# First norm and first two projection blocks worked in two token halves

## What is computed

```python
def rms_norm(x, g):
    xf = x.astype(jnp.float32)
    y = xf * lax.rsqrt(jnp.mean(xf * xf, axis=-1, keepdims=True) + EPS)
    return (y * g.astype(jnp.float32)).astype(x.dtype)
...
        h = rms_norm(x, norm1_g[l])
        z = jnp.einsum('bsd,de->bse', h, w_in[l])
        lru_x, lru_gate, sc_b, sc_c, sc_x = jnp.split(z, splits, axis=-1)
        lru_x = causal_dwconv(lru_x, lru_conv_w[l]) + lru_conv_b[l]
```

## Time and profile before

| | |
|---|---|
| median of the runs | 1700.8 us |
| span of the profiled execution | 1699.3 us |
| TensorE busy | 1670.6 us, 98% of the span |
| VectorE, ScalarE, GpSimd busy | 74%, 46%, 27% |
| first matmul of the projections | 26.49 us from the start |
| first matmul of the third block | 50.63 us |

### The profile page before, as it was taken

One profiled execution on the slowest core, in us unless ns is written; L12 is line 12 of the kernel. 1 busy time (PEld: TensorE's weight loads), 2 busy tenths in 40 slices (PEclk: granted clock), 3 DMA queues, 4 the chain that ended last, 5 costly groups with the idle time before them and its releaser, 6 DMA issues.

```text
span 1699.3 us, 20967 instructions
## 1 busy us (share of the span) xinstructions
PE 1670.6 (98%) x7556; PEld 1381.3 (81%) x7556; DVE 1261.6 (74%) x1490; ACT 780.3 (46%) x1048; POOL 451.8 (27%) x270
## 2 busy tenths in 40 slices
PE   6999999999999999999999999999999999999998
PEld 5888878888887888888888888888888888788786
DVE  7577772258999888888888788889827846777654
ACT  5566551225764343434344454555432317566531
POOL 4222222200006455545554000004523342300000
PEclk9999999999999999999999999999999999999999
DMA  8111112143413322222221884852322231020351
GB/s 263 50 37 49 37 50 65 48 166 107 146 69 90 94 74 86 91 82 74 85 83 59 309 306 134 261 189 82 109 87 62 62 111 32 10 78 26 108 224 71
DMA packets 161095, 176.96 MB, mean 104 GB/s; under 512 B 13566, under 2 KB 114692, under 8 KB 161028
## 3 DMA queue, kind: packets, MB, share of 16 engines
q1 hardware_dynamic: 158724, 167.67, 30.6%
q10 hardware_dynamic: 2304, 8.39, 1.3%
HBM read 140.38 MB, written 35.65 MB: 104 GB/s over the span
## 4 chain that ended last, share of the span: by engine, by line
PE 90%; DVE 6%; ACT 2%; issue 1%; DMA 0%; POOL 0%; DVEq 0%
PE ps L950 31%; PE ps L2517 26%; PE ps L2471 19%; PE ps L2763 5%; PE ps L2748 3%; PE ps L2599 1%; PE ps L2802 1%; PE ps L2720 1%; DVE pt_lo L2324 1%; DVE prob L2281 1%; PE ps L2736 1%; DVE square_dve L1707 0%; ACT pt_hi L1606 0%; PE ps L2620 0%; DVE pair_sum L1913 0%
## 5 line engine op out<-in xcount | busy, mean ns | idle before, releaser
L974 POOL TENSOR_TENSOR w_lo<-w_raw,w_hi 128x1024 fp32r<-128x1024 f32 x52 | 134.6, 2591 | 624.9 <-ACT w_hi L1081 624.9
L2517 PE MATMUL ps<-hop_hi_P,wop_hi_P 128*128 128x512 f32 x672 | 263.6, 392 | 3.2 <-DVE u L1924 2.5
L2517 PE MATMUL ps<-hop_lo_P,wop_hi_P 128*128 128x512 f32 x672 | 262.9, 391 | 0.0
L2517 PE MATMUL ps<-hop_hi_P,wop_lo_P 128*128 128x512 f32 x672 | 262.7, 391 | 0.0
L950 PE MATMUL ps<-h_hi,w_hi 128*128 128x512 f32 x720 | 224.1, 392 | 7.5 <-DVE h_lo L1692 6.0
L980 POOL TENSOR_TENSOR wop_lo_P<-pair_sum,wop_hi_P 128x512 fp32r<-128x512 f32 x90 | 136.4, 1516 | 355.4 <-ACT wop_hi_P L1092 355.4
L950 PE MATMUL ps<-h_lo,w_hi 128*128 128x512 f32 x720 | 222.6, 390 | 0.0
L950 PE MATMUL ps<-h_hi,w_lo 128*128 128x512 f32 x720 | 222.2, 390 | 0.0
L950 PEld LDWEIGHTS ps<-h_hi,w_hi 128*128 128x128 f32 x720 | 135.1, 189 | 36.9 <-issue 9.4
L950 PEld LDWEIGHTS ps<-h_lo,w_hi 128*128 128x128 f32 x720 | 135.7, 189 | 28.4
L950 PEld LDWEIGHTS ps<-h_hi,w_lo 128*128 128x128 f32 x720 | 135.7, 188 | 28.3
(11 more groups left out here) (363 smaller groups left out, 3348.9 us busy)
## 6 DMA issues: line engine op xcount, KB each, us to landing
pair_raw<-in_w_up SPq DMA_DIRECT2D x48, 512.0 KB, 4.8
w_raw<-in_w_in SPq DMA_DIRECT2D x46, 512.0 KB, 3.9
dn_raw<-gu_park SPq DMA_DIRECT2D x84, 256.0 KB, 3.9
dn_raw<-in_w_down SPq DMA_DIRECT2D x60, 256.0 KB, 3.1
gu_park<-up_cv SPq DMA_DIRECT2D x24, 512.0 KB, 2.6
out_raw<-in_w_out SPq DMA_DIRECT2D x30, 256.0 KB, 3.1
x_tok<-in_x SPq DMA_DIRECT2D x4, 1024.0 KB, 8.2
x_park<-xs SPq DMA_DIRECT2D x1, 4096.0 KB, 14.3
```

Of the source, the lines that this page charges most:

```text
L974: nc.gpsimd.tensor_tensor(lo[:, :], raw[:, :], hi[:, :].bitcast(f32), ALU.subtract).then_inc(w_lo_done, 1)
L2517: mm = nc.tensor.matmul(dst, w[q][:, k, :], x[q][:, k, :], start=a, stop=b, skip_group_check=True)
```

## The change

The norm and the first two blocks are done for tokens 0 to 511 (`T1`) and then for tokens 512 to 1023 (`T2`).

- SyncE's queue: x parts 0 and 1, the two weight blocks, then x parts 2 and 3. The 16 row transfers go to ScalarE's queue, in front of ScalarE's own work; a square root of a constant stands behind them. The rows now lie in the second half of the `scr` tiles' space, which the `T2` half of the norm uses.
- Factors come in two sets of four token blocks. VectorE squares blocks 0 to 3 first, then 4 and 6 between tiles of `T1`; ScalarE squares 5 and 7.
- Every normed tile, `h_hi` and `h_lo` is made in two halves of 512 tokens.
- TensorE: 32 transposes, the first rows, the first spread, 16 transposes, then block steps of three matmuls for `T1`, with the last 16 transposes, the other rows and the second spread between them, then the steps for `T2`. Block 0 counts as done after its `T2`.
- GpSimd, not ScalarE, rounds the first weight block (`w_hi[0]`).
- The semaphore counts further on (`v_done`, `hi_done`, `rstd_done`, `rb_done`) are shifted to match; the work there is the same.

```diff
+        ROWS_FIRST, ROWS_LATE = 16 * 12, 16 * 4
+        XT_COPIED = (1, 2, 3, 4, 5, 7, 8, 10)
+        FIRST_V, FIRST_LOW = 2 * KT, KT
...
-            for n in range(4):
+            def x_load(n):
                 sp.dma_start(x_tok[:, 2 * n:2 * n + 2, :], x_v[:, 2 * n:2 * n + 2, :]).then_inc(x_in[n], 16)
...
-                sp.dma_start(rows0[row:row + n, 0:P], v).then_inc(rows_in, 16)
...
+            x_load(0)
+            x_load(1)
...
             for b in range(2):
                 load(N_LRU + b, 0, (cols(b, 8, P), w_in_v[:, :, b * D:b * D + P]))
+            x_load(2)
+            x_load(3)
...
-            sp.wait_ge(xt_copied, NT)
+            sp.wait_ge(xt_copied, XT_COPIED[NT - 1])
             sp.dma_start(x_park.rearrange("c p t -> p c t"), xs[:, :, :]).then_inc(x_parked, 16)
...
+            pool.wait_ge(w_in_sem[0], 16)
+            nc.gpsimd.tensor_copy(w_hi[0][:, :], w_raw[0][:, :]).then_inc(w_hi_done, 1)
             low(0)
             low(1)
-            odd_lows(0, lambda c: scr[c % 4][:, :])
+            odd_lows(0, T1)
+            odd_lows(1, T2)
...
+            act.dma_start(rows1[0:72, :], ffn_rows[0:72, :]).then_inc(pos_in, 16)
+            act.dma_start(rows2[0:72, :], ffn_rows[72:144, :]).then_inc(pos_in, 16)
+            act.dma_start(pos_rows_i[0:NT, :], positions_2.rearrange("o (n p) -> (o n) p", p=P)
+                          ).then_inc(pos_in, 16)
+            act.dma_start(freq[:, :], rope_freq).then_inc(pos_in, 16)
+
+            act.wait_ge(const_done, SMALL_CONST)
+            nc.scalar.activation(small[:, 47:48], eps[:, 0:1], ACT.Sqrt).then_inc(sumsq, 1)
 
             def xt_copy(t):
 
                 act.wait_ge(xt_done, t + 1)
-                nc.scalar.copy(xs[:, :, t * P:(t + 1) * P], ps[t % 3][:, :].rearrange("p (c q) -> p c q", c=KT)
-                               ).then_inc(xt_copied, 1)
-
-            for t in range(NT - 2):
...
+            for t in range(3):
                 xt_copy(t)
-
-            act.wait_ge(x_in[3], 16)
-            nc.scalar.activation(scr[4][:, :], x_tok[:, NT - 1, :], ACT.Square,
-                                 accum_out=small[:, NT - 1:NT]).then_inc(sumsq, 1)
-            act.wait_ge(sumsq, 1)
-            act.wait_ge(sumsq_dve, NT - 1)
-            act.wait_ge(const_done, SMALL_CONST)
-            nc.scalar.activation(small[:, 8:16], small[:, 0:8], ACT.Sqrt, bias=eps[:, 0:1],
-                                 scale=1.0 / D).then_inc(root_done, 1)
-            xt_copy(NT - 2)
-            xt_copy(NT - 1)
             act.wait_ge(vec_t, 1)
-            nc.scalar.copy(vec[:, :], ps[3][:, 0:V_COLS]).then_inc(vec_done, 1)
-            high(0)
+            nc.scalar.copy(vec[:, 0:V_ROWS], ps[3][:, 0:V_ROWS]).then_inc(vec_done, 1)
+            token_root(0)
+            xt_copy(3)
+            act.wait_ge(w_hi_done, 1)
             high(1)
-            highs(lambda c: scr[c % 4][:, :], lambda c: (v_done, c + 1))
+            normed_high(0, T1)
+            normed_high(1, T1)
+            xt_copy(4)
+            normed_high(2, T1)
+            normed_high(3, T1)
+            xt_copy(5)
+            normed_high(4, T1)
+            token_square(5, 1)
+            normed_high(5, T1)
+            xt_copy(6)
+            normed_high(6, T1)
+            xt_copy(7)
+            normed_high(7, T1)
+            token_square(7, 2)
+            token_root(1)
+            act.wait_ge(vec_t, 2)
+            nc.scalar.copy(vec[:, V_FFN:V_COLS], ps[3][:, V_FFN:V_COLS]).then_inc(vec_done, 1)
+            for c in range(KT):
+                normed_high(c, T2)
...
+            for t in range(4):
+                token_square(t, t)
+            token_factor(0)
+            dve.wait_ge(pos_in, ROWS_LATE)
             V.tensor_copy(pos_rows[0:NT, :], pos_rows_i[0:NT, :]).then_inc(setup_done, 1)
             dve.wait_ge(vec_done, VEC)
+            dve.wait_ge(xt_copied, XT_COPIED[3])
             dve.wait_ge(rb_done, 1)
-            dve.wait_ge(xt_copied, NT)
-            norm(0, V_NORM1, lambda c: scr[c % 4][:, :], ps[2][:, :], True)
-
+            normed(0, T1)
+            for c in range(KT):
+                if c + 1 < KT:
+                    normed(c + 1, T1)
+                if c % 2 == 0:
+                    even_low(c, T1)
+                if c in (3, 6):
+                    token_square(4 if c == 3 else 6, 4 if c == 3 else 5)
+            token_factor(1)
+            dve.wait_ge(xt_copied, XT_COPIED[NT - 1])
+            dve.wait_ge(rb_done, 2)
+            normed(0, T2)
+            for c in range(KT):
+                if c + 1 < KT:
+                    normed(c + 1, T2)
+                if c % 2 == 0:
+                    even_low(c, T2)
+            dve.wait_ge(vec_done, VEC_ALL)
...
                 if t >= 3:
-                    pe.wait_ge(xt_copied, t - 2)
+                    pe.wait_ge(xt_copied, XT_COPIED[{3: 0, 4: 2, 5: 3, 6: 4, 7: 5}[t]])
...
+            for t in range(4):
+                by_channel(t)
+            pe.wait_ge(rows_in, ROWS_FIRST)
+            by_column(rows0, V_ROWS, 0).then_inc(vec_t, 1)
             pe.wait_ge(rstd_done, 1)
-            spread(ps[2]).then_inc(rb_done, 1)
...
-            first_two(0, (ps[0], ps[1]), 0)
+            spread(ps[3], range(4), HALF).then_inc(rb_done, 1)
+            by_channel(4)
+            by_channel(5)
+
+            def first_step(b, j, t):
+
+                if t is T1 and j == 0:
+                    pe.wait_ge(w_lo_done, b + 1)
+                if b == 0:
+                    pe.wait_ge(lo_dve if j % 2 == 0 else lo_pool, 4 * (t is T2) + j // 2 + 1)
+                wh, wl = blocked(b)
+                for w, x, first, last in ((wh, h_hi, j == 0, False), (wh, h_lo, False, False), (wl, h_hi, False, j == 7)):
+                    mm = nc.tensor.matmul(ps[b][:, t], w[:, j, :], x[:, j, t], start=first, stop=last)
+                if j == 7 and t is T2:
+                    mm.then_inc(block_done, 1)
+
+            def first_blocks(k, t):
+                for b, j in ((0, k), (1, k - 3)):
+                    if 0 <= j < 8:
+                        first_step(b, j, t)
+
+            pe.wait_ge(xt_copied, XT_COPIED[3])
+            for k in range(8 + 3):
+                first_blocks(k, T1)
+                if k == 3:
+                    by_channel(6)
+                elif k == 4:
+                    by_channel(7)
+                elif k == 5:
+                    pe.wait_ge(pos_in, ROWS_LATE)
+                    pe.wait_ge(setup_done, POS_F)
+                    by_column(rows1, 72, V_FFN)
+                    by_column(rows2, 72, V_FFN + 72)
+                    by_column(pos_rows, NT, V_POS).then_inc(vec_t, 1)
+                elif k == 8:
+                    pe.wait_ge(rstd_done, 2)
+                    pe.wait_ge(xt_copied, XT_COPIED[NT - 1])
+                    spread(ps[2], range(4, NT)).then_inc(rb_done, 1)
+            for k in range(8 + 3):
+                first_blocks(k, T2)
```

## The result

The changed kernel takes 1704.9 us (median of 8 runs, 1703.7 to 1706.6) against 1700.8 (8 runs, 1699.7 to 1701.4): a ratio of 1.0026, 95% interval 1.0017 to 1.0035. That is inside the range, but slower by a little more than the 0.2% that I had called no change (the interval reaches down to 0.17%). The mechanism that I forecast took place; 3.3 us came on top of the forecast of 1701.6.

A forecast was written before the change was run, and what follows sets the result against it. TensorE bounds the kernel (90% of 1699.3 us). Third block -0.8 and half clock +1.6 give +0.8, span 1700.1; with the median 1.5 above the span, 1701.6 us, range 1698.3 to 1705.5.

The forecast's parts named there:

- rival B: Slower: TensorE granted half clock through most of T1, about +10 us, 1711; chance 0.12.
- Rival C: Slower: first tile late through GpSimd (+1.9) or rows (+3.6); a 6 us first call would give 1707; chance 0.10.
- half-width operations take 0.68 alone, 0.61 in a row ... 7.4, end at 39.85: VectorE's T2 norm: 8 norm tiles and 4 rests from 32.4 take 7.4 us; parameters then end at 44.6.
- Some 4.4 us early: TensorE at block 1's end is some 4.4 us early, of which 3.6 becomes a new idle stretch.
- 12 tile products ... waits 1.0: 43.5: TensorE's T2: from the first rest at 34.3, products at 0.68 plus waits end block 0 at 43.5.
- +1.6, bounds 0 and 2.7: Half clock on TensorE behind the new idle stretch before the third block costs 1.6 us.
- rival A: Faster: T1 runs without waits, third block at 48.3, clock holds: -2.3, 1698.5; chance beyond 0.2%: 0.10.
- TensorE bridges many short waits at 1.00 between 31.0 and 50.6: Argument for rival A from the trace of before: TensorE's clock holds at 1.00 through short waits.
- No later cover: Behind the third block TensorE is the chain, so the +0.8 there reaches the end: span 1700.1.
- The median's distance from the span: The runs' median lies 1.5 us above the profiled span, turning 1700.1 into 1701.6.
- Rule weighed: VectorE's two squares in T1's waits stand up to 1.2 us each behind GpSimd; otherwise third block 0.4 earlier, 1701.2.
- My 1.3: GpSimd's rounding of w_hi[0] takes 1.3 us, between bounds of 0.95 and 2.34.

The follow-up runs named there:

- both edits: Changed kernel with early parameters, the second half's block 0 ahead of block 1, and the second spread one tile step earlier: 1700.4 us, 0.9999 of the kernel before.
- early parameters: Changed kernel with twelve small parameter operations and the exponential moved ahead of the second half's norm: 1702.7 us, 1.0014 of the kernel before.
- block 0 ahead of block 1: Changed kernel whose second half does all eight tiles of block 0, then all eight of block 1: 1704.5 us, 1.0020 of the kernel before.
- cast late: Changed kernel with VectorE's cast of the positions moved behind the first rest of the first half: 1705.8 us, 1.0031 of the kernel before.
- rows alone: Kernel before with only the 16 row transfers moved from SyncE's to ScalarE's queue, ahead of its copies: 1701.8 us, 1.0008 of the kernel before.
- x first: Changed kernel with all four parts of x asked for ahead of the first weights: 1711.7 us, 1.0069 of the kernel before.
- better version: Both edits, but series steps back behind the second norm, last two squares and second root earlier, second spread at k == 6: 1699.0 us, 0.9992 of the kernel before.
- filled: Changed kernel plus 16 unread matmuls in TensorE's idle stretch before the third block: 1702.3 us, 1.0010 of the kernel before.
- one-tile lag: Kernel before with block 1 following block 0 by one tile instead of three: 1705.5 us, 1.0029 of the kernel before.
- changed again: Changed kernel once more, unchanged, for a second profile: 1704.7 us, 1.0024 of the kernel before.
- better version again: The better version once more, unchanged: 1698.5 us, 0.9988 of the kernel before.

## Why the prediction was right or wrong

**Right: what bounds the start.** First matmul 17.9 (forecast 18.2), second spread ends at 32.3 (32.3), second half's norm at 32.42 (32.4), parameters last, then an idle stretch of 3.68 (3.6) and the clock at 0.50 behind it. The gain in front is given back at the convolution: shown by the version with both edits, which brings 1.8 us at the third block, where early parameters alone bring 0.6 and block 0 ahead of block 1 alone brings nothing that its faster front does not explain. The idle stretch fits because both its ends came 0.9 late: block 1 ended at 47.07 (46.2), the third block began at 50.75 (49.8).

**The time was inside the range by luck.** The range reached up to 1705.5 through a rounding of 2.34 on GpSimd (1.71 measured), the clock at 2.7 (1.6 in the first profile) and a little of rival B, which did not come. What brought the time there were four others, given here for the changed kernel's first profile: 0.9 at the third block, 1.0 around 490 us, 0.8 at 1613 us and 0.5 outside the span. Slower by more than 0.2% had a chance of 0.22, through B and C; neither was the way.

**Wrong by 0.8: "half-width operations take 0.68 alone, 0.61 in a row ... 7.4, end at 39.85".** No row shows the 0.61. Two norm tiles and a rest took 1.40 + 0.69 with small gaps, 2.04 in all or 0.68 each, and four of these 8.2 us until 40.6. In the kernel before, three full-width operations took 3.53 (26.27 to 29.80), 1.18 each: halving the width did not halve the time. The parameters came 0.8 later (45.41). From `half_ba` to `kx` it took 3.4, and `half_ba` ended 1.2 behind its start because of GpSimd, both as forecast.

**A slip in the sum.** Convolution at 44.65 and the same 5.3 behind it give 49.95, not 49.8, and -0.7 instead of -0.8; with the 0.8 above this is the +0.1 that was measured. "Some 4.4 us early" is 4.1 by its own terms.

**Wrong, without effect: "12 tile products ... waits 1.0: 43.5".** Block 0 was ready at about 44.8, as the start of the convolution with early parameters shows, 0.6 ahead of the parameters. **Nor had the sum the cast of the positions**, which stood 2.14 us and moved the first half's norm to 14.90 (forecast 13.6); the run with the cast late shows that this held nothing back but 0.3.

**The clock, "+1.6, bounds 0 and 2.7".** In the first profile exactly 1.6, in others 2.4, 2.6 and 2.7 of the same idle stretch; that the first one hit the number is chance. Filling the stretch takes it away. Of the profiles here, the four with 3.67 or 3.68 us of idle time in front of the third block fell and those with 2.33, 2.70 and 3.04 held, but 1.96 and 2.01 us at 13 to 15 us fell, and 1.78 held. The length of the wait alone does not decide, and I read no threshold from so few executions.

**A row misread in favour of rival A: "TensorE bridges many short waits at 1.00 between 31.0 and 50.6".** That stretch holds no wait; TensorE is busy all through it:

```profile
...
31.00:50.60 19.60, 19.60 (x87) 15.91 (x85) 15.09 (x29) 8.15 (x9) 8.47 (x4) 1.00 0.23 63
...
```

**Missing from the sum: "No later cover".** It holds, but further losses do not follow: +1.0 or +1.5 around 490 us. There TensorE runs at half clock in stretches in every profile of every kernel. They cost as much as in the kernel before in both its profiles and in four others (rows alone, both edits, x first, better version), 1.0 more in four (changed, filled, early parameters, one-tile lag) and 1.5 more in four (changed again, cast late, block 0 first, better version again). They are two short ones, one long one, or a short and a long one. The same kernel shows 1.0 and 1.5, or 0 and 1.5, so the size is of the execution. All of them lie at or right behind two runs of one-column matmuls, which no kernel here changes. Whether moving the front makes the dear cases likelier stays open.

**Near 1613 us** the changed kernel's chain waits for a transfer:

```profile
...
1600.08 10.19 DMA zin<-y_park
...
```

It is not in the chain of the same kernel's second profile, and costs between 0 and 1.0 over all profiles, against the first one of before: by that a chance of the landing, of which that profile had next to none.

**The median's distance from the span** was taken as 1.5 and is 1.75 to 1.87 in the later runs of the kernel before: my sum was 0.3 short there. The other 0.2 is the changed kernel's; it is in all its variants, the rows' queue alone does not make it, and its cause is open.

Sum for the medians: 0.1 at the third block, 1.6 to 2.4 by the clock behind it, 1.0 to 1.5 around 490, 0.2 outside, and 0 to 0.8 by the landing: 3 to 5, measured 4.1.

**Rule weighed.** The two squares behaved as the trace of before let expect: one stood behind GpSimd (1.81), one ran alone (1.22). The Trainium skill, "SBUF — State Buffer", section "Who interferes with whom", says that whoever starts first holds the ports for the whole instruction. It agrees in both directions here: GpSimd's rounding of the weights took 1.71 when it began 0.8 us before the end of a square on VectorE, and 1.04 in the version with x in one piece, where VectorE was idle. My 1.3 lay between; by the same page's rule the estimate would have been that wait on top of the bound of 0.95, 1.75. That the rounding took 0.4 more did no harm, since the subtractions behind it ended at 17.2, before the 17.9 that I had for them.

**Rival C's first call** did not happen: the first rounding on GpSimd took 1.71 in the changed kernel and 1.04 in the version with x in one piece. The Trainium skill, "GPSIMD Engine Reference", section "Instruction dispatch", has about 6 us for it; no run here shows it.

## What to carry to other kernels

Starting earlier pays only as far as what follows is ready: read which wait ends last behind the moved work (here parameters and block 0, 0.6 us apart), and move all that are that close together. Splitting work into halves takes cover from behind the first block, so order the second half by who is waited for, and keep TensorE from standing in front of a dense stretch. Where the whole effect is a few microseconds, take two profiles of each kernel before a loss far behind the change is laid to it.

## What the hardware showed

A cast of 8x128 on VectorE took 2.14 and 1.30 us while GpSimd worked, and 0.21 with GpSimd idle (in the version with x in one piece): a small operation, too, stands until GpSimd's instruction under way has ended (14.88 for the cast that ended at 14.96).

Behind an idle stretch of the same length, 3.68 us, the half clock covered 3.4 us in one execution of a kernel; in the next it covered 6.7 us (49.1 to 55.8) and began inside the idle stretch. The mean granted clock over the span (0.994 to 0.997) tells how much half clock a run had, but not where: the profiled run with block 0 first has 0.995 with the clock at 1.00 behind the third block's start.

The two transfers of weights took SyncE 7.03 us to issue right behind four of x (version with x in one piece), and 3.56 behind two (changed kernel).
